# One attention stage instead of two in a fp32 two-block model: pairs of heads of both kinds in turn, the latents' norms moved into it, the query norms applied in the exponential

## What is computed

```
proj = h @ w_in
cq, ckv, kpe, fq, fk, fv, fl = split(proj, (384, 256, 32, 512, 512, 512, 8))
q_a  = (rms_norm(cq, mla_qa_g) @ w_uq).reshape(b, s, 8, 96)
kv_a = (rms_norm(ckv, mla_kva_g) @ w_ukv).reshape(b, s, 8, 64 + 64)    # k_nope, v_a
k_a  = concat(k_nope, kpe of every head)
q_a, k_a = rms_norm(q_a, mla_q_g), rms_norm(k_a, mla_k_g)              # per head, 96 wide
q_a, k_a = rope on the last 32 of both
o_a  = causal_attention(q_a, k_a, v_a, 96 ** -0.5)
q_b, k_b = rms_norm(fq, fox_q_g), rms_norm(fk, fox_k_g)                # per head, 64 wide
fcum = cumsum(log_sigmoid(fl + b_f))
o_b  = causal_attention(q_b, k_b, fv, 64 ** -0.5, fcum)                # + fcum[t] - fcum[s]
x    = x + gate1 * (concat(o_a, o_b) @ w_o)
```

## Time and profile before

| | |
|---|---|
| median of 3 runs | 3084.47 us (3081.39 to 3085.98) |
| the profiled execution's own time | 3083.38 us |
| its span | 3081.6 us |
| TensorE (PE) busy over the span | 2484.2 us, 81% |
| VectorE (DVE) busy | 2154.5 us, 70% |
| ScalarE (ACT), GpSimd (POOL) busy | 1006.6 us, 1190.1 us |
| mean granted TensorE clock | 0.909 of 2.4 GHz |

### The profile page before, as it was taken

The page is one execution under the profiler, slowest core; times in us unless marked ns, Lnnn a source line. Parts: engine busy times, 40 slices in busy tenths (PEclk is TensorE's granted clock), DMA queues, the critical chain, the costliest instruction groups (busy, mean ns, idle before and its releaser), DMA issues. The chain is left out here.

```text
span 3081.6 us, 36160 instructions
## 1 busy us (share of the span) xinstructions
PE 2484.2 (81%) x12224; PEld 1695.7 (55%) x12224; DVE 2154.5 (70%) x3952; ACT 1006.6 (33%) x2029; POOL 1190.1 (39%) x971
## 2 busy tenths in 40 slices
PE   6998969999999798678899798766676667766665
PEld 5998969999999694244566443322222222222222
DVE  6346856777777885576334477777777878778776
ACT  2223135666666322233233222222222221222221
POOL 1444456666666430111003133443434344434442
PEclk8999989999999898787999999988889888888888
DMA  3233621221111162000301499999999999999998
GB/s 103 79 102 98 191 82 56 62 61 54 54 56 54 48 191 68 22 8 1 82 1 48 185 382 418 406 421 406 421 421 418 394 421 421 416 394 421 421 421 337
DMA packets 269756, 666.40 MB, mean 216 GB/s; under 512 B 13989, under 2 KB 201546, under 8 KB 203834
## 3 DMA queue, kind: packets, MB, share of 16 engines
q0 software_dynamic: 73728, 536.90, 42.2%
q1 hardware_dynamic: 194906, 127.75, 14.1%
q10 hardware_dynamic: 992, 0.13, 0.0%
HBM read 662.64 MB, written 2.10 MB: 216 GB/s over the span
## 5 line engine op out<-in xcount | busy, mean ns | idle before, releaser
L2106 PE MATMUL peer_py<-peer_uv,peer_diag 128*128 128x512 f32 x1536 | 841.6, 695 | 362.1 <-ACT peer_diag L2026 361.7
L1794 POOL DMA_INDIRECT peer_uv<-k_peer_uv,peer_idx x512 | 501.0, 978 | 772.6 <-PE peer_py L2106 727.9
L1906 DVE SCALAR_TENSOR_TENSOR peer_spare<-peer_uv,peer_hp 128x1024 bf16<-128x1024 f32 x512 | 622.4, 1217 | 236.5 <-DMA peer_uv<-k_peer_uv,peer_idx 236.3
L2106 PEld LDWEIGHTS peer_py<-peer_uv,peer_diag 128*128 128x128 f32 x1536 | 320.4, 221 | 844.4 <-issue 837.1
L2018 ACT ACTIVATE peer_ga<-peer_a 128x2 f32<-128x2 f32 x256 | 52.0, 203 | 843.8 <-DVE peer_spare L1906 843.8
L890 POOL TENSOR_TENSOR hgrn_wl<-p2n_w,hgrn_wh 128x1024 fp32r<-128x1024 f32 x64 | 152.5, 2393 | 231.7 <-ACT hgrn_wh L927 231.7
L1023 PE MATMUL hgrn_pp<-p2n_hh,hgrn_wh 128*128 128x264 f32 x1024 | 219.0, 295 | 17.5 <-POOL p2n_hl L340 16.7
L1023 PE MATMUL hgrn_pp<-p2n_hh,hgrn_wl 128*128 128x264 f32 x1024 | 209.6, 286 | 0.0
L1023 PE MATMUL hgrn_pp<-p2n_hl,hgrn_wh 128*128 128x264 f32 x1024 | 209.6, 286 | 0.0
L2026 ACT ACTIVATE peer_diag<-keep_ident,peer_wt 128x128 f32<-128x128 f32 x384 | 140.1, 396 | 112.1 <-DVE peer_wt L1915 111.5
L1023 PEld LDWEIGHTS hgrn_pp<-p2n_hh,hgrn_wh 128*128 128x128 f32 x1024 | 160.1, 191 | 20.7 <-issue 14.6
(11 more groups left out here) (396 smaller groups left out, 4867.2 us busy)
## 6 DMA issues: line engine op xcount, KB each, us to landing
p2n_w<-in_hgrn_w_in SPq DMA_DIRECT2D x64, 512.0 KB, 4.0
p1n_w<-in_pool_w_in SPq DMA_DIRECT2D x32, 512.0 KB, 4.0
pool_out_aw<-in_w_ada SPq DMA_DIRECT2D x16, 768.0 KB, 4.7
hgrn_out_aw<-in_w_ada SPq DMA_DIRECT2D x16, 768.0 KB, 4.9
pool_out_w<-in_pool_w_out SPq DMA_DIRECT2D x8, 1024.0 KB, 7.5
p_w<-in_w_pq SPq DMA_DIRECT2D x8, 1024.0 KB, 16.0
peer_uv<-k_peer_uv,peer_idx POOLq DMA_INDIRECT x512, 12.4
fox_wq<-in_w_in SPq DMA_DIRECT2D x12, 512.0 KB, 6.4
```

The lines of the kernel that those rows point to most:

```text
L1794: pool.indirect_dma_start(out=uv[:, n % DEPTH].rearrange("p w d -> p (w d)"), out_offset=None, in_=io["k_peer_uv"], in_offset=bass.Indirec ...
L1906: dve.scalar_tensor_tensor(out=spare[:, n % 2, :], in0=uv[:, n % DEPTH, 0, :], scalar=1.0, in1=hp[:, t % 2, :], op0=ALU.mult, op1=ALU.mult ...
L2106: last = pe.matmul(py[:, h * 512:(h + 1) * 512], diag[:, products(n) % DIAGS, :], uv[:, n % DEPTH, 1, h * 512:(h + 1) * 512], start=n % (P ...
```

## The change

The two calls of `heads_phase` become one `attention_phase` of eight pairs, fox at even places and mla at odd ones, so that fox units carry the entries of an mla pair and mla units those of a fox pair. The first lead-in is that of a fox pair, and there is one. The latents' sums, roots and scalings move from the end of `latent_phase` to the start of the new stage; TensorE issues the latents' sums ahead of that lead-in, which does not read the latents. In `latent_phase` the gate tile is computed first, the residual copy goes behind the angles, and the squares go to `oT`. The first weights of both kinds are loaded during `latent_phase`; later ones into a single buffer for each kind, once the pair before of that kind has its values. For mla, the rotation reads the projection before its norm (the gains are folded into `turn` and `cos`), the key's inverse root multiplies at the end, and the query's inverse root, one number for each query, becomes the exponential's scale and a factor of the maximum (L1709 of the new kernel). The query's sums of squares are then four products with one column each. The diff, cut:

```
-            pe.wait_ge(w_in, 32)
...
+            for kind, m in tiles:
+                rows = {"f": AH, "k": QK, "l": P}[kind]
+                pe.wait_ge(wl_in if kind == "f" else w_in, 16)
...
+                    last = pe.matmul(pr[0:rows, m, :], lhs, hm[:, k, :], start=k == 0, stop=k == KC - 1)
                 last.then_inc(summed, 1)
...
-            pe.wait_ge(taken, n_lat)
-            for j, (a, b) in enumerate(((0, n_cq), (n_cq, n_lat))):
-                pe.wait_ge(squared, b)
-                for m in range(a, b):
-                    last = pe.matmul(pr[:, j, :], keep["ones"][:, :], sq[:, m, :], start=m == a, stop=m == b - 1)
-                last.then_inc(sum_done, 1)
...
+                act.activation(la["lat"][:, m, :], pr[:, m, :], ACT.Copy)
+                act.activation(oT[:, m, :], pr[:, m, :], ACT.Square)
...
             norm.dve(dve)
-            norm.residual(dve)
...
+            dve.wait_ge(summed, 1)
+            ch.link(dve.tensor_scalar(z[:, :], pr[0:AH, 6, :], gains[0:AH, G_BF:G_BF + 1], None, ALU.add))
...
-            for j, (a, b, name) in enumerate(((0, n_cq, "mla_qa_g_2"), (n_cq, n_lat, "mla_kva_g_2"))):
-                dve.wait_ge(rooted, j + 1)
-                ch.link(dve.reciprocal(rs[:, j, :], rs[:, j, :]))
-                for m in range(a, b):
-                    c = COL[name] + m - a
-                    ch.link(dve.scalar_tensor_tensor(out=la["lat"][:, m, :], in0=raw[:, m, :], scalar=cols[:, c:c + 1],
-                                                     in1=rs[:, j, :], op0=ALU.mult, op1=ALU.mult))
+            norm.residual(dve)
             dve.wait_ge(ln_done, 1)
...
+def attention_phase(nc, io, keep, la, hm, oT, wm, wkv, wf, wm_in, wf_in):
...
+        raw, sq = ph.sb("raw", [P, 4, SEQ]), ph.sb("sq", [P, 4, SEQ])
+        rs, rsq = ph.sb("rs", [P, 2, SEQ]), ph.sb("rsq", [P, 2, TT])
+        fraw, fsq, frs = (ph.sb(s, [P, 2, SEQ]) for s in ("fraw", "fsq", "frs"))
+        turn, cos = ph.sb("turn", [P, 2, QK]), ph.sb("cos", [P, 2, SEQ])
+        qk, fqk = ph.sb("qk", [P, 4, SEQ]), ph.sb("fqk", [P, 3, SEQ])
...
+        M_SLOTS = [[("raw", 0), ("raw", 2)], [("raw", 1), ("raw", 3), ("rot", 0)], [("ones", r) for r in order],
+                   [("rot", 2), ("v", 0)], [("rot", 1)], [("rot", 3)], [], []]
+        M_DVE = [[], [("rot", 0)], [], [("norm", 0), ("norm", 1), ("norm", 2), ("rot", 2)], [("norm", 3), ("rot", 1)],
+                 [("rot", 3)], [], []]
+        F_SLOTS = [[("raw", 0)], [("raw", 1)], [("ones", 0), ("ones", 1)], [("v", 0)], [], [], [], []]
+        F_DVE = [[("right", 0)], [("right", 1)], [("norm", 0)], [("norm", 1)], [], [], [], []]
...
+            for p in range(2, N):
+                i = p // 2
+                if mla[p]:
+                    sp.wait_ge(filled, place[p - 2, "v", 0] + 1)
...
+                elif kind == "ones" and not mla[p]:
+                    pe.wait_ge(fsquared, i * 2 + (r + 1))
+                    last = pe.matmul(to, la["pair"][:, :], fsq[:, r, :], start=True, stop=True)
+                elif kind == "ones":
+                    pe.wait_ge(squared, i * 4 + (order.index(r) + 1))
+                    if r < 2:
...
+                            last = pe.matmul(to[:, t:t + 1], sq[0:QK, r, t * P:(t + 1) * P], keep["ones"][0:QK, 0:1],
+                                             start=True, stop=True)
                     else:
-                        pe.wait_ge(nrm_done, j * n_raw + (order.index(r) + 1))
-                        last = pe.matmul(to[0:QK, :], la["rot"][:, :], nrm[0:QK, r, :], start=True, stop=True)
-                    last.then_inc(filled, 1)
+                        last = pe.matmul(to[0:QK, :], keep["ones"][0:QK, 0:QK], sq[0:QK, r, :], start=True, stop=True)
+                else:
+                    if p == 1:
+                        pe.wait_ge(gain_done, 4)
...
+                    pool.wait_ge(*taken((p, "raw", r)))
+                    if i:
+                        pool.wait_ge(filled, place[p - 2, "ones", r] + 1)
+                    pool.tensor_tensor(sq[0:QK, r, :], raw[0:QK, r, :], raw[0:QK, r, :], ALU.mult).then_inc(squared, 1)
+                    if i == 0:
+                        pool.wait_ge(gain_done, 4)
+                    pool.tensor_tensor(qk[0:QK, r, :], raw[0:QK, r, :], cos[0:QK, r // 2, :], ALU.mult)\
...
+                n, u = (g % TT + 1) * P, g % U
+                scale = rsq[:, u // TT, g % TT:g % TT + 1] if mla[g // U] else 1.0
                 act.wait_ge(nm_done, g + 1)
-                act.activation(pr_[:, g % 2, 0:n], pS[:, g % 2, 0:n], ACT.Exp, bias=nm[:, g % U:g % U + 1],
...
+                act.activation(pr_[:, g % 2, 0:n], pS[:, g % 2, 0:n], ACT.Exp, bias=nm[:, u:u + 1], scale=scale,
+                               accum_out=sums[:, u:u + 1]).then_inc(e_done, 1)
...
+            for i, (a, b, n, name) in enumerate(latents):
+                act.wait_ge(lat_summed, i + 1)
+                act.activation(raw[:, i, :], pT_[:, i, :], ACT.Sqrt, bias=keep["eps"][:, 0:1], scale=1.0 / n)\
+                   .then_inc(lat_rooted, 1)
...
+            for i, g in enumerate((G_Q, G_K)):
+                gain = gains[0:QK, g:g + 1]
+                act.activation(turn[0:QK, i, :], la["rot"][:, :], ACT.Copy, scale=gain).then_inc(gain_done, 1)
+                act.activation(cos[0:QK, i, :], la["cos"][:, :], ACT.Copy, scale=gain).then_inc(gain_done, 1)
...
+                    elif kind == "norm" and mla[p]:
+                        dve.wait_ge(*taken((p, "ones", r)))
+                        root = rsq[:, r, :] if r < 2 else rs[0:QK, r - 2, :]
+                        ch.link(dve.reciprocal(root, root))
...
+                        e = (p, "rot", r)
+                        dve.wait_ge(filled, place[e] + 1)
+                        dve.tensor_tensor(tmp[0:QK, :], bank(e)[0:QK, :], la["sin"][:, :], ALU.mult).then_inc(v_taken, 1)
+                        dve.wait_ge(*taken(e))
+                        dve.wait_ge(cos_done, i * 4 + (order.index(r) + 1))
+                        ch.link(dve.tensor_tensor(qk[0:QK, r, :], qk[0:QK, r, :], tmp[0:QK, :], ALU.add))
+                        if r >= 2:
+                            ch.link(dve.tensor_tensor(qk[0:QK, r, :], qk[0:QK, r, :], rs[0:QK, r - 2, :], ALU.mult))
                         dve.sem_inc(qk_done, 1)
...
+                ins = dve.tensor_reduce(to, pS[:, g % 2, 0:n], AX_X, ALU.max, negate=True)
+                if mla[g // U]:
+                    ch.link(ins)
+                    ins = dve.tensor_tensor(to, to, rsq[:, u // TT, g % TT:g % TT + 1], ALU.mult)
+                ins.then_inc(nm_done, 1)
...
+            ch.link(dve.memset(fqk[:, 0:2, :], 0.0))
+            for i, (a, b, n, name) in enumerate(latents):
+                dve.wait_ge(lat_rooted, i + 1)
+                ch.link(dve.reciprocal(raw[:, i, :], raw[:, i, :]))
+                for m in range(a, b):
+                    c = COL[name] + m - a
+                    dve.scalar_tensor_tensor(out=la["lat"][:, m, :], in0=la["lat"][:, m, :], scalar=cols[:, c:c + 1],
+                                             in1=raw[:, i, :], op0=ALU.mult, op1=ALU.mult).then_inc(lat_done, 1)
             walk(entries, unit)
...
+                        def latent_ahead(sp):
+                            view = io["w_in_2"].rearrange("(k p) n -> p k n", p=P)
+                            sp.dma_start(wl[:, :, :], view[:, :, FL_AT:IN_W]).then_inc(wl_in, 16)
+                            sp.dma_start(w[:, :, :], view[:, :, 0:FQ_AT]).then_inc(w_in, 16)
+                            for m, at in enumerate((FQ_AT, FK_AT, FV_AT)):
+                                sp.dma_start(wf[:, m], view[:, :, at:at + P]).then_inc(wf_in, 16)
+                            sp.dma_start(wm[:, :, :], io["w_uq_2"].rearrange("(k p) n -> p k n", p=P)[:, :, 0:2 * QK])\
+                              .then_inc(wm_in, 16)
+                            sp.dma_start(wkv[:, :, :], io["w_ukv_2"].rearrange("(k p) n -> p k n", p=P)[:, :, 0:4 * FD])\
```

More of the change, by code:

```diff
@@ L1281, in latent_phase @@
         pr = ph.ps("pr", [P, 8, 512])
[L1282 to L1285, removed]
+        k_in, summed, own, z_done, ex_done, ln_done, red_done = (
+            ph.sem(s) for s in "k_in summed own z_done ex_done ln_done red_done".split())
         norm = NormPair(keep, ph, keep["hT"][:, :, META:T], keep["xT"], hm, keep["total"], weighted, pr[:, 6:8, :])
         blk = ph.block()
-        gains, cols = keep["gains"], keep["cols"]
+        gains = keep["gains"]
+        tiles = [("f", 6), ("l", 3), ("l", 4), ("k", 5), ("l", 0), ("l", 1), ("l", 2)]
         @blk.sync
@@ new lines, in attention_phase @@
+        F_DVE = [[("right", 0)], [("right", 1)], [("norm", 0)], [("norm", 1)], [], [], [], []]
+        seq = [(p, *e) for p in range(N) for slot in (M_SLOTS if mla[p] else F_SLOTS) for e in slot]
+        place = {e: g for g, e in enumerate(seq)}
+        by_act = {e: i for i, e in enumerate(e for e in seq if e[1] != "rot")}
```

(26 more changed lines are left out.)

357 lines of the change are left out of this document (159 added, 198 removed).

## The result

The changed kernel takes 3007.28 us (median, 3003.33 to 3010.02) against 3082.93 beside it: ratio 0.9754, 95% interval 0.9742 to 0.9765. Run again later it took 3005.37, ratio 0.9749 (0.9736 to 0.9762). The forecast was 3006. The profiled execution took 3003.33, the fastest of the four.

A forecast was written before the change was run, and what follows sets the result against it. Mla periods were taken as bound by one VectorE queue, fox periods by TensorE. Gains of 15.5 (latents' end), 50.3 (lead-in, loads) and 12.7 (periods), 78.5 in all, gave 3004.9 profiled; median 1.1 above, 3006; range 2985 to 3041.

The forecast's parts named there:

- Latents: End of the latents' stage: moved work and early weight loads cost 0; the new stage starts at 1239.9.
- my 15.5 us: Share of the 78.5 us gain booked to the latents' end, before the attention stage.
- Lead-in: Start of the attention stage: one lead-in, no DMA wait, 31.1 us, first exponential at 1271.0.
- A: Four periods of fox units with mla entries: 41.0 us each, the first 38.
- the forecast's own signs: Attention stage: among others PEclk 1.00 throughout; clock near 0.5 behind unit 3 in fox units with mla entries would show it wrong.
- Rival (a): TensorE's clock falls in fox units with mla entries: some 9 us more each, + 36, 3042; chance 0.12.
- rival (b): Three VectorE instructions per fox period with mla entries stretched by 1 us through GpSimd's lock: + 12, 3018; chance 0.10.
- B: Three periods of mla units with fox entries: 39.9, say 40 us each.
- Tail: Last mla pair, without entries, at the attention stage's end: 22.5 us.
- 12.7 from the periods: Rest of the 78.5 us gain, booked to the periods after the latents' end, hidden lead-in and loads.

The follow-up runs named there:

- single fox buffer: Changed kernel with pair order (four fox, then four mla) and query norms both undone, one buffer for fox's weights: 3042.5 us, ratio 0.9865.
- blocks: Changed kernel with four fox pairs, then four mla pairs, new query norms: 3026.1 us; with two buffers for fox's weights 3020.49 us.
- one-bank kernel: Changed kernel with the sums of both queries of an mla pair in one bank: 3001.71 us, ratio 0.9739.
- early key: Changed kernel with query 0's and key 0's sums and roots and key 0's inversion a slot earlier, first rotation a slot later: 2992.61 us, ratio 0.9711.

## Why the prediction was right

The forecast said 3006; 3007.3 and 3005.4 came. By its steps:

- **Latents (right).** The stage's first product in the profiled execution came at 1235.5 for 1239.9, but 2.3 to 2.7 of these 4.4 us are drift from earlier stages: the same instruction stands at 1237.8, 1238.1 and 1238.2 in three other executions with the same latents' stage. VectorE waited 0.40 us on the small transfers, so eight transfers ahead of them cost next to nothing. Of my 15.5 us, 4.3 reappear as sums in the lead-in; the 11.2 left were measured as 9.5 to 11.4.
- **Lead-in (right).** 30.3 us for 31.1, without a DMA wait; the early weights alone are worth 5.4 to 7.3.
- **A (mechanism right, term too small).** 41.0 forecast; 42.7, 44.0, 42.8, and 39.6 for 38. To unit 1's transposes 15.2 (14.7), to unit 2's 7.1 (6.3), the rest 20.3 (20.0). I had seen the bank's wait, and taken 1.9 for all of slot 2. More than half of the excess goes with the clock: an A other than the first takes 41.85 at 1.00, 42.5 to 43.3 at 0.96 and 43.7 to 44.0 at 0.92 over the executions of this order. At 1.00 that is 0.85 above the forecast; the three are 1.7, 3.0 and 1.8 above. Two of the forecast's own signs failed with this: the clock was not 1.00 over the stage, and it was 0.50 for a time behind unit 3 in three of four A. Rival (a) came true in small, 1 to 2 us an A and not 9; rival (b) too: two VectorE instructions an A are stretched, by 0.17 and 0.58 us and not three by 1 each, and undoing the 0.58 brings unit 2 forward by as much. The Trainium skill (SBUF — State Buffer, section Who interferes with whom) names VectorE instructions with two SBUF inputs, and scalings in a mode with two ports, as those that can meet GpSimd's at a shared port, and calls it an exclusive lock: the later one waits out the earlier. The trace agrees, if what counts is what is left of the earlier one: the addition lost 0.17 of the 0.31 us left of the square, the scaling 0.58 of the 0.78 left of the product. In the kernel before, a scaling began 0.03 us behind the product, and lost nearly all of it, 1.52 for 0.48:

```profile
1367.31 1.26 POOL L1587 TENSOR_TENSOR mla_qk<-mla_nrm,p_cos 96x512 f32<-96x512 f32 x1 [7.50 <-DVE mla_nrm L1668]
1367.34 1.52 DVE L1693 TENSOR_SCALAR mla_p<-mla_p,mla_sums 128x512 f32<-128x512 f32 x1
```

- **B (right).** 40.04 and 40.05 for 40.
- **Tail.** 20.1 for 22.5: I took the mla pair's 21.2, part of which was a clock of 0.92.
- **The split of the gain** was booked in a way that hides its parts. "12.7 from the periods" (12.5: the lead-ins give 81.6 less 31.1, 50.5 and not 50.3) nets one more loaded period in place of a tail against shorter ones. By the runs: one lead-in, early weights and latents' norms bring 39.6 us with a single fox buffer (3082.05 to 3042.47), 45.2 without its cost of 5.6; the query norms in blocks 16.3; the alternation 13 to 15. Sum 75 to 77, measured 75.7 and 77.7. That they add up proves nothing, for each is the difference of two runs in one chain; the split depends on the order of undoing (the norms are worth 22.5 to 24.4 in alternation), and with key 0's inversion early the alternation is worth 2.6 us or nothing.

From the first exponential to the stage's end it took 309.2 us for 303.5: the four A 8.0 over, the tail 2.4 under, the rest nothing. That stretch began 5.2 us earlier than forecast, half of it drift. And the profiled execution lay 3.95 us below the median, where 1.1 was assumed. The hit within 2 us is in good part luck: these errors cancelled.

## What to carry to other kernels

Price a mixed order against the same order with its longest serial step moved first: here moving one inversion of 3.35 us (with its sum and root, which also ended a wait for a bank) into a slot where VectorE waited for projections gave as much as alternating the pairs, and left the alternation with hardly any worth. When a stage is merged away, book the period that replaces its tail; a remainder that looks like "shorter periods" hides it. Judge edits of a few us by marks within a period, counted from its start and at equal clock: there 0.6 and 0.9 us could be told apart, while medians and sums of periods could not rank the edits.

## What the runs showed of the hardware

- TensorE's granted clock fell to 0.50 in A behind waits of 0.77 or 1.83 us (score products over 128 columns 0.64 us for 0.39), by a different amount in each period of one execution (0.92 or 0.96 in the mean), and the same waits also passed without a fall: a wait of 1.83 in an A of the one-bank kernel left it at 1.00. With the early key it was 1.00 in all eight.
- VectorE and GpSimd instructions that overlapped lost time on both sides: a scaling 0.58 us with 0.78 left of GpSimd's product, 1.04 with 1.23 left, and a GpSimd product beside an addition 0.45 (1.26 to 1.71).
- The exponential with a scale operand of one value a partition took 0.457 us for 128 columns against 0.367 without. The Trainium skill (ScalarE: Activation LUTs, section What ACT_TABLE_LOAD costs) gives about 93 ns for each operand of one value a partition; the trace agrees.
